# Prompt attention over eight heads: the next head's query, key and value units between the current head's row blocks

## What is computed

```python
q    = rms_norm(x @ wq_a) @ wq_b            # 384 -> 8 x (128 + 64)
q_pe = rope(q[..., 128:])                   # rotary part, 64 columns
s    = q_nope @ k_nope.T + q_pe @ kpe.T     # k_nope = ckv @ wkv_b[:, h, :128]
p    = softmax(mask(s * SM_SCALE))          # causal, 1040 keys
o[h] = p @ (ckv @ wkv_b[:, h, 128:])        # values, 128 columns
```

## Time and profile before

| | |
|---|---|
| runs before | 2707.92, 2709.01, 2711.21 us; median 2709.01 |
| the profiled execution | 2707.35 us, its span 2705.5 us |
| TensorE busy in the span | 2454.9 us (91%) |
| VectorE, ScalarE, GpSimd busy | 1298.0, 773.7, 357.1 us |
| mean granted clock of TensorE | 0.953 of 2.4 GHz |

### The profile page before, as it was taken

The page is one execution under the profiler, slowest core; times in us unless marked ns, Lnnn a source line. Parts: engine busy times, 40 slices in busy tenths (PEclk is TensorE's granted clock), DMA queues, the critical chain, the costliest instruction groups (busy, mean ns, idle before and its releaser), DMA issues.

```text
span 2705.5 us, 36839 instructions
## 1 busy us (share of the span) xinstructions
PE 2454.9 (91%) x14022; PEld 2228.9 (82%) x14022; DVE 1298.0 (48%) x2463; ACT 773.7 (29%) x1451; POOL 357.1 (13%) x288
## 2 busy tenths in 40 slices
PE   7899999999999777888887888899999999999994
PEld 7799999999998576777776666677989999999993
DVE  4523333333333755564565777745143333333336
ACT  2331111111111324444444555522311111111112
POOL 2400000000000600000003555314000000000006
PEclk9899999999999888998998999989999999999998
DMA  4121111111110121000002544440111111111111
GB/s 152 39 63 48 46 39 39 47 47 47 47 55 20 49 88 33 1 16 16 0 1 88 154 138 145 136 140 16 32 51 44 47 47 47 47 47 47 47 40 63
DMA packets 133769, 153.24 MB, mean 57 GB/s; under 512 B 10064, under 2 KB 109936, under 8 KB 133544
## 3 DMA queue, kind: packets, MB, share of 16 engines
q1 hardware_dynamic: 121392, 110.07, 13.1%
q0 software_dynamic: 12288, 41.95, 5.0%
HBM read 142.24 MB, written 10.32 MB: 56 GB/s over the span
## 4 chain that ended last, share of the span: by engine, by line
PE 75%; DVE 11%; issue 5%; ACT 5%; POOL 2%; DMA 2%; ACTq 0%; SPq 0%; POOLq 0%; DVEq 0%
PE ps L214 22%; PE ps L215 21%; PE ps L216 21%; DVE split L207 5%; ACT split L202 2%; PE ps L1776 2%; PE ps L1811 2%; DVE plain L290 1%; POOL plain L338 1%; POOL plain L340 1%; PE ps L222 1%; PE ps L221 1%; PE ps L1401 1%; PE ps L1791 1%; PE ps L1792 1%
## 5 line engine op out<-in xcount | busy, mean ns | idle before, releaser
L214 PE MATMUL ps<-split 128*128 128x344 f32 (+9 forms) x3632 | 1255.4, 346 | 106.9 <-DVE split L207 60.7
L215 PE MATMUL ps<-split 128*128 128x344 f32 (+9 forms) x3632 | 1237.1, 341 | 0.0
L216 PE MATMUL ps<-split 128*128 128x344 f32 (+9 forms) x3632 | 1236.1, 340 | 0.0
L214 PEld LDWEIGHTS ps<-split 128*128 128x128 f32 x3632 | 703.0, 194 | 164.8 <-issue 48.7
L216 PEld LDWEIGHTS ps<-split 128*128 128x128 f32 x3632 | 703.6, 194 | 38.0
L215 PEld LDWEIGHTS ps<-split 128*128 128x128 f32 x3632 | 703.8, 194 | 36.9
L202 ACT ACTIVATE split<-plain 128x344 fp32r<-128x344 f32 (+8 forms) x430 | 312.0, 758 | 646.7 <-PE ps L222 405.8
L207 DVE TENSOR_TENSOR split<-plain,split 128x1024 fp32r<-128x1024 f32 (+7 forms) x422 | 356.1, 867 | 196.5 <-ACT split L202 193.3
L274 DVE TENSOR_TENSOR plain<-plain,ps 128x512 f32<-128x512 f32 (+2 forms) x396 | 268.4, 685 | 202.3 <-PE ps L216 196.9
L207 DVE TENSOR_TENSOR split<-ps,split 128x512 fp32r<-128x512 f32 (+6 forms) x476 | 247.1, 558 | 203.9 <-ACT split L202 201.2
L910 DVE TENSOR_TENSOR plain<-plain,ps 128x350 f32<-128x350 f32 (+1 forms) x132 | 68.0, 515 | 567.8 <-ACT plain L866 567.2
(11 more groups left out here) (144 smaller groups left out, 1450.0 us busy)
## 6 DMA issues: line engine op xcount, KB each, us to landing
plain<-w_gate SPq DMA_DIRECT2D x44, 512.0 KB, 4.8
plain<-w_up SPq DMA_DIRECT2D x44, 512.0 KB, 4.0
plain<-w_down SPq DMA_DIRECT2D x44, 512.0 KB, 4.4
plain<-x_prompt SPq DMA_DIRECT2D x8, 512.0 KB, 11.4
x_spill<-plain SPq DMA_DIRECT2D x1, 4096.0 KB, 18.1
plain<-wo SPq DMA_DIRECT2D x8, 512.0 KB, 4.8
plain<-x_spill SPq DMA_DIRECT2D x8, 512.0 KB, 8.2
y_prompt<-plain SPq DMA_DIRECT2D x8, 512.0 KB
```

The source lines that it names most:

```text
L214: pe.matmul(out, still[0], moving[0], start=start, stop=False)
L215: pe.matmul(out, still[0], moving[1], start=False, stop=False)
L216: return pe.matmul(out, still[1], moving[0], start=False, stop=stop)
```

## The change

The loop over pairs goes; 64 row blocks m = 8h + n are one list, and the units of the next head are placed in it by tables. Only a prologue of 12 units stands in front: both rotary units of pair 0, query and key of head 0, all values of pair 0.

In an even head h, the units of head h + 1 and the rotary units of the next pair are placed; in an odd head, those of h + 1 and the first four value units of the next pair, the fifth (one tile) in block 0 of head h + 1. A place is EARLY (after `scores`), MID (before the third fill of the turn) or LATE (after the turn). A value unit now makes two tiles in one bank, split with two to four small operations. Queries and keys keep two buffers (head even, odd), values three. ScalarE does `exp(m)` before the turned splits, except at n = 1. `values` waits first for all fills but the last and for the last one only where it is used. Each unit waits for the unit that had its bank before, and the scores of wide blocks wait for units in banks 4, 1 and 2. The rotary query is made in two steps: rotation at its unit, the split for head h at block 1 of the head before. Weights are split per head (`split_own`, at block 7 of head h for h + 2), per pair for rotary (block 2 of even heads) and values (block 7 of even heads), and loaded in those pieces. Zero padding of the values is eight memsets in place of four.

```diff
-UNITS = [("qn", 0, 0), ("qn", 0, 1), ("qp", 0, 0), ("kn", 0, 0), ("kn", 0, 1), ("qp", 0, 1), ("kn", 0, 2)] + \
-        [("v", 0, t) for t in range(9)] + \
-        [("qn", 1, 0), ("qn", 1, 1), ("kn", 1, 0), ("kn", 1, 1), ("kn", 1, 2)]
+PROLOGUE = [("qp", 0, 0, 0), ("qp", 0, 1, 1), ("qn", 0, 0, 2), ("kn", 0, 0, 3), ("v", 0, 0, 4), ("qn", 0, 1, 6),
+            ("kn", 0, 1, 0), ("v", 0, 1, 1), ("kn", 0, 2, 2), ("v", 0, 2, 3), ("v", 0, 3, 4), ("v", 0, 4, 6)]
+EARLY, MID, LATE = 0, 1, 2
+FOR_ODD = {(1, MID): ("kn", 0, 4), (2, LATE): ("qn", 0, 4), (3, MID): ("kn", 2, 4), (3, LATE): ("kn", 1, 2),
+           (4, LATE): ("qn", 1, 2), (5, LATE): ("qp", 0, 2), (6, EARLY): ("qp", 1, 2)}
+FOR_EVEN = {(1, MID): ("kn", 0, 4), (1, LATE): ("qn", 0, 2), (2, EARLY): ("v", 0, 1), (3, EARLY): ("qn", 1, 4),
+            (3, LATE): ("kn", 1, 2), (4, LATE): ("v", 1, 2), (5, EARLY): ("v", 2, 2), (5, LATE): ("v", 3, 2),
+            (6, EARLY): ("kn", 2, 2)}
...
+def split_times(eng, k, h, n, act):
+
+    if n == 2 and h % 2 == 0 and h + 2 < k.heads:
+        split_rotary(eng, k, h // 2 + 1, act)
+    if n == 7 and h + 2 < k.heads:
+        split_own(eng, k, h + 2, act)
+        if h % 2 == 0:
+            split_values(eng, k, h // 2 + 1, act)
```

TensorE's list (`heads_pe`):

```diff
+    for m in range(8 * k.heads + 3):
+        h, n = m // 8, m % 8
+        if h < k.heads:
+            scores(h, n)
+            if h % 2 == 0 and n == 3:
+                sample_latent_queries(h // 2)
+        placed_unit(h, n, EARLY)
+        if n % 2 == 0 and m >= 4:
+            values((m - 4) // 2)
+        if 2 <= m < 8 * k.heads + 2:
+            turn(m - 2, 0)
+            turn(m - 2, 1)
+        placed_unit(h, n, MID)
+        if 2 <= m < 8 * k.heads + 2:
+            turn(m - 2, 2)
+        placed_unit(h, n, LATE)
+        if h < k.heads and h % 2 == 0 and n == 1:
+            sample_queries(h // 2)
```

ScalarE's list (`heads_act`):

```diff
+    for m in range(8 * k.heads + 3):
+        h, n = m // 8, m % 8
+        turns = 2 <= m < 8 * k.heads + 2
+        if n == 1 and turns:
+            turned(m - 2, 0)
+        if h < k.heads:
+            exp(m)
+        unit(unit_at(k, h, n, EARLY))
+        if n % 2 == 0 and m >= 4:
+            out((m - 4) // 2)
+        if turns:
+            if n != 1:
+                turned(m - 2, 0)
+            turned(m - 2, 1)
+        unit(unit_at(k, h, n, MID))
+        if turns:
+            turned(m - 2, 2)
+        unit(unit_at(k, h, n, LATE))
+        if h < k.heads:
+            if n == 1 and h % 2 == 0:
+                sample_queries(h // 2)
+            if n == 1 and h + 1 < k.heads:
+                rotary_query(h + 1)
+            split_times(act, k, h, n, True)
```

VectorE's list (`heads_dve`):

```diff
+    for m in range(8 * k.heads + 2):
+        h, n = m // 8, m % 8
+        turns = m >= 2
+        if 1 <= m <= 8 * k.heads:
+            normalise(m - 1)
+        if h < k.heads:
+            row_max(m)
+        if h < k.heads and h % 2 == 0 and n == 3:
+            sample_latent_queries(h // 2)
+        unit(unit_at(k, h, n, EARLY))
+        if turns:
+            turned(m - 2, 0)
+            turned(m - 2, 1)
+        unit(unit_at(k, h, n, MID))
+        if turns:
+            turned(m - 2, 2)
+        unit(unit_at(k, h, n, LATE))
+        if h < k.heads and n == 1:
+            if h % 2 == 0:
+                sample_queries(h // 2)
+            if h + 1 < k.heads:
+                rotary_query(h + 1)
```

More of the change, by code:

```diff
@@ L1414, in values @@
         slots = [(b, b) for b in range(2 * gp + 2)] + [(2 * gp + 2, EXTRA_SLOT)]
-        cols = slice(h * P, (h + 1) * P)
-        for m, (b, slot) in enumerate(slots):
-            mm = product(pe, out, (k.v[:, 0, b, cols], k.v[:, 1, b, cols]),
-                         (k.pt[:, 0, slot, :], k.pt[:, 1, slot, :]), m == 0, m == len(slots) - 1)
-        mm.then_inc(s["pv_done"], 1)
[L1421 to L1425, removed]
-            if n == 13:
-                sample_latent_queries(j)
-        for n in range(19):
-            if n < 16:
-                scores(j, n)
-            if n >= 4 and n % 2 == 0:
-                values(j, n - 3)
-            if 2 <= n < 18:
-                turn(j, n - 2)
-        pe.wait_ge(s["exp_done"], 16 * (j + 1))
-        pe.wait_ge(s["pt_lo"], NR * (j + 1))
-        pe.wait_ge(s["o_copied"], 8 * (j + 1))
@@ L1498, in heads_act, with out @@
+    def out(g):
+        h, gp = g // 4, g % 4
+        act.wait_ge(s["pv_done"], g + 1)
+        act.activation(k.ot[:, h, gp * 256:(gp + 1) * 256], k.ps[:, 7, 0:256], ACT.Copy).then_inc(s["o_copied"], 1)
     act.wait_ge(s["spilled"], 16)
     act.wait_ge(s["lat_lo"], latent_tasks(k))
[L1500 to L1516 removed]
@@ L1518, in heads_act @@
-    pairs_of(act, k, pair)
-def turned_view(k, g, n, place, slot, count):
-    cols = slice((n % 2) * P, (n % 2 + 1) * P)
+    act.wait_ge(s["extra_zero"], 8)
+    split_rotary(act, k, 0, True)
+    split_own(act, k, 0, True)
+    split_values(act, k, 0, True)
+    for u in PROLOGUE:
+        unit(u)
+        if u[:3] == ("kn", 0, 0):
+            rotary_query(0)
+    split_own(act, k, 1, True)
+    for m in range(8 * k.heads + 3):
[22 more added lines that the diff above has]
+            split_times(act, k, h, n, True)
@@ L1523, in turned_view @@
+def turned_view(k, g, m, place, slot, count):
+    cols = slice((m % 2) * P, (m % 2 + 1) * P)
     src = k.ps[:, 5 + g % 2, place * P:(place + count) * P].rearrange("p (b n) -> p b n", b=count)
@@ new lines, in unit @@
+            dve.tensor_tensor(rotated, rotated, k.swapped[t], ALU.add).then_inc(s["qp_steps"], 1)
+            return
+        if kind == "v":
+            before = value_ops_before(k, h, t)
+            parts = list(values_parts(k, h, t, bank))
+            dve.wait_ge(s["v_hi"], before + len(parts))
+            for n, (src, hi, lo) in enumerate(parts):
+                lo_part(dve, lo, src, hi).then_inc(s["v_lo"], 1)
+            dve.wait_ge(s["v_lo"], before + len(parts))
+            dve.sem_inc(s["hd_unit_lo"], 1)
+            return
```

580 lines of the change are left out of this document (356 added, 224 removed).

## The result

The changed kernel takes 2767.67 us (median of 4 runs, 2764.17 to 2776.59), the kernel before 2709.35 (4 runs): a ratio of 1.022, 95% interval 1.0193 to 1.0246. It is 58 us slower. The forecast was 12.6 us faster, and its range ended at 2714.

The account below looks back on a forecast made before the run. Bound: TensorE's work plus waits for VectorE and slow clock. Stage 23.5 + 290.3 + 3 x 9.1 + 3 x 6.0 + 8.2 + 21 + 21 = 409.3 against 421.9, 12.6 us less: 2696.4, range 2668 to 2714.

Parts of the forecast that it names:

- the schedules above: Engine queues of the attention stage followed in code order with measured durations; they gave 9.1 us an even head, 6.0 an odd.
- 27.3 + 18 + 8.2 + 21 + 21: Three even heads at 9.1 us, three odd at 6.0, blocks 1 to 4, slow clock stretches, then heads 6 and 7.
- blocks 1 to 4: Scores held by units' splits at these blocks: 0.95 us four times and 1.45 three times, 8.2 us.
- their old losses: Heads 6 and 7: one change of head 6.7 us, dense part about 3, one end 10 to 11; 21 us.
- Start: Prologue of units with its slow stretch and last splits: block 0 starts 23.5 us after 1028.6.
- Steps: TensorE's matmul and transpose work in the stage, none removed: 308 us, 290.3 of it after the prologue.
- Rotary units: In heads 0, 2, 4, ScalarE's four copies hold VectorE, so TensorE waits 1.9 and then 3.2 us a head.
- Value units: In odd heads value unit 3 waits 2.2 us for unit 2's bank; the first holds block 3's scores, 1.1 + 0.35.
- the odd heads: Heads 1, 3, 5: TensorE's waits at value unit 3, block 7's scores, values and turns, 6.0 us a head.
- Clock: Each wait over 1.7 us brings a 1.6 us slow stretch: 3.5 us a head, 21 in six; clock about 0.93.
- the clock stays down: Rival: slow stretches merge from qp 0 to the next head's block 2, 6.5 us a head for 3.5; 2714; chance 0.12.
- units only fill holes: Rival: heads with units take the old 31.35 us period plus units' steps; stage 387 us, total 2674; chance 0.20.

Follow-up runs that it names:

- kernel 1: The changed kernel with ScalarE's early unit, copy of the values' result and first two turned splits put before exp(m), as TensorE orders them: 2674.60 us, ratio 0.9861.
- 5: The kernel before with only ScalarE's order changed as the change does it, exponential first: 2788.07 us, ratio 1.030.
- 8: The changed kernel with turned splits and the copy of the values' result before exp(m), the early unit still behind it: 2712.08 us, one run.
- 9: The changed kernel with the early unit ahead of the exponential and the turned parts left behind it, except block 1's first: 2743.61 us, one run.
- Kernel 2: The changed kernel with a third probabilities buffer in heads 0 to 4 and value unit 0 split behind the copy of the values' result: 2739.24 us, ratio 1.010.
- 4: The changed kernel with 128 semaphore increments on TensorE between decode and projection: 2764.54 us, ratio 1.0202.
- 6: The kernel before with its loop over three pairs of heads written out: 2702.59 us, ratio 0.9969.
- 7: kernel 1 with 128 semaphore increments at the start of TensorE's list: 2671.04 us, ratio 0.9853 to the kernel before.
- 12: kernel 1 with 64 semaphore increments at the start of TensorE's list: 2658.24 us, ratio 0.9802 to the kernel before.
- 3: The changed kernel with ScalarE's four copies in each rotary unit cut from 512 columns to 8: 2745.22 us, one run.
- 10: kernel 1 with the swap copies of the rotary queries cut from 512 columns to 8: 2668.61 us, one run.
- 11: kernel 1 with a third buffer of probabilities for blocks 0 to 39: 2679.03 us, ratio 0.9885 to the kernel before.

## Why the prediction was wrong

*The step that failed* is the sentence "The exponential now stands before the turned splits in ScalarE's list; it is in the schedules above". In those schedules the exponential waited for the maximum alone. It also waits for the transposes of block m-2, as it did in the old kernel, and with that I should have seen that it comes late by its own queue and takes the unit's and the turn's high parts with it. Kernels 1, 5, 8 and 9 show it: 85 us of the stage in the new schedule, 79 in the old one. In the sum, the waits and slow stretches of the blocks were 95.5 us (27.3 + 18 + 8.2 + 21 + 21); in the whole stage, with those of the start, they measured 150.0.

The wait alone was not the whole miss. Kernel 2, with that wait a block further back in five heads, has a stage of 441.0 us where my sum had 409.3. I charged blocks 1 to 4 of six heads 8.2 us in all and the last heads their old losses; head 7 alone lost 9.3 us more than before, by the order and nothing else.

*Start*: 23.5 us until block 0 was near; its scores start at 1050.42, 21.8 us in. *Steps*: 308 us of work came out at 303. *Rotary units*: the waits of 1.9 and 3.2 us a head, 15.3 in three heads, were 18.3 in six waits, of 1.66 and 4.44. The size was near, but most of it wasn't the copies' own: in kernel 1, with every copy still made, the two waits are 1.15 and 0.80, 5.8 us in all, and leaving the copies out gave about 10 us of the stage. *Value units*: the wait of value unit 3, 2.2 us in my sum, is 2.55; block 3's scores wait 2.42 for 1.45. But the odd heads as a whole were too cheap: between 1234 and 1270 us head 3 has five waits of 11.3 us in all, for 7.5. *Clock*: 0.90 for a forecast of 0.93. In the kernel before, the slower clock cost 30.8 us of the stage, 38.3 after and 15.3 in kernel 1, worked out from the starts of matmuls: it goes with the waits (78.8, 111.7 and 51.2 us, counted in the same way), and it is 7.5 us of the 38.5 that the stage grew by. The rival "the clock stays down" had its sign to show, a period of two heads of 104 us or more at a clock under 0.88; the period is 116.0 at 0.882, long enough but not quite under that clock, and kernel 1 takes waits and slow stretches away together by the order alone.

*The second feed-forward* was no term at all, +15.5 us. That another length of TensorE's list ahead of a loop can cost time in the loop was costed at nothing.

*The rival "units only fill holes"* was where the design lies without the order: it had 387 us for the stage and kernel 1 has 376. Against it I had put "the queues' order above"; the real order did much more harm than I charged, and with the one that fits the stage comes out under that figure.

The rule that I weighed, that ScalarE and VectorE are strict first-in, first-out queues (the Trainium skill, "TensorE: Matmul & The Clock Gate", section "Architectural detail: the array is 16× 32×32, not 1× 128×128"), agrees with the trace: the high part whose input was ready at 1239.4 stood behind the exponential while ScalarE was idle until 1239.85, and started at 1240.54. I used the rule for VectorE's maximum and didn't follow it for ScalarE's exponential.

## What to carry to other kernels

When an instruction is moved forward in an engine's list, write down every semaphore that it waits for, the reuse of its own output buffer among them, and ask for each instruction that is now behind it who needs it sooner. Where engines hand work to each other in a ring, give the later ones the order in which the first one produces; here that was worth 3.4% by itself, more than the whole pipeline. Compare stages that the diff doesn't touch as well, and with them the packets of the instruction queue: a change in the length of a program can move a later loop into a worse place.

## What was not expected of the hardware

Eight kernels have a second feed-forward of 786 to 800 us, and six, the old ones and those with 64 or 128 increments ahead, of 777 to 780. The fetches of 16 KB in the stage (queue q8) and TensorE's "issue" waits in it put all fourteen in one order:

| kernels | fetches | "issue" waits, us | 2nd feed-forward, us |
|---|---|---|---|
| before, 4, 5, 6, 7, 12 | 14 | 4.3 | 777.3 to 779.9 |
| 3 | 23 | 8.7 | 785.9 |
| after, 8, 10, 11 | 32 | 12.3 to 13.7 | 790.4 to 793.6 |
| 1, 2, 9 | 41 | 16.8 to 17.2 | 796.6 to 799.6 |

So the time goes up by 6 to 7 us for each 9 fetches. In after, the two places with waits for "issue" besides the one that all kernels have (at 2137.6 and 2140.5, and at 2282.3 and 2285.2) lie a round of the loop apart: none, one, two or three rounds are fetched again. The eight slow kernels have TensorE lists of the same length and order, since their edits change only ScalarE's order, the width of the copies or the probabilities' buffer; so by these runs the place of the code decides whether rounds are fetched again, and not how many. This is also the 6.9 us of kernel 3. TensorE's code for a round of the loop is some 1630 to 1690 instructions of 64 bytes, about 6.5 pieces of 16 KB (my count from the trace). In kernel 4 TensorE stood 15.97 us at its 128 increments, 0.12 us for each, of which 12.4 us were left at the end of the projection.

The Trainium skill, "Runtime: NRT & Kernel Launch", section "Instruction fetch mechanics", gives TensorE 128 KiB, 2048 instructions, for its code, filled in blocks of 16 KiB with the next one fetched ahead. By that figure such a loop touches 7 blocks or 8, by where it starts in a block, and with one ahead 8 or 9 for 8 places, an estimate. The runs agree with it in that the fetches come and go with a shift of a quarter of a block; which places are bad was not tried out further, and that this is the cause of the 15.5 us is shown so far as the shift removes the fetches and the time together, and the time follows the number of fetches.

What remains open: what decides how many rounds are fetched again with the same list of TensorE, which engine's code the fetches carry (the queue's packets don't tell), and what more the stage's 376 us would give, of which 303 are steps.
